# A float32 two-block network on one core: the delta-rule inverse in 64-row blocks, modulation tiles in three slots, distances on ScalarE, latent items in pairs

## The reference

```python
# layer 0, per head and chunk: (I + L) x = rhs, L strictly lower triangular
lower = where(strict, einsum("bhncd,bhnkd->bhnck", kb, k) * decay, 0.0)
sol = triangular_solve(lower, rhs, lower=True, unit_diagonal=True)
...  # then a scan over the chunks with state (dk x dv), and o -> rms_norm(o) * silu(z)

# second block: modulation of the norms
mod = silu(c) @ ada_w + ada_b            # (1024) @ (1024, 6144)

# second block: top 256 keys by an index score, logits with a bucketed bias
rel = pos_sel - pos_b
side = where(rel > 0, 16, 0); n = abs(rel)
bucket = side + (n if n < 8 else log-spaced, steps at 12, 16, 23, 32, 46, 64, 91)
logits = q . kv_sel * scale + rel_bias[bucket]
probs = softmax(logits); out = probs @ kv_sel
```

## Time and profile before

| what | us |
|---|---|
| median of three runs | 3050.55 (3041.01 to 3058.16) |
| profiled execution, time | 3044.59 |
| profiled execution, span of the core | 3042.8 |
| inverse, on PE | 263.6 to 371.0 |
| transposes, then recurrence from its first vn product | 371.0 to 377.2 to 407.3 |
| sums of squares | 407.3 to 418.3 |
| modulation columns | 418.3 to 435.0 |
| gating and memory attention, to the first product of wout0 | 435.0 to 483.5 |
| last gab unit done; first latent product; last | 2033.1; 2042.8; 2240 |

### The profile page before, as it was taken

One profiled execution on the slowest core, in us unless ns is written; L12 is line 12 of the kernel. 1 busy time (PEld: TensorE's weight loads), 2 busy tenths in 40 slices (PEclk: granted clock), 3 DMA queues, 4 the chain that ended last, 5 costly groups with the idle time before them and its releaser, 6 DMA issues.

```text
span 3042.8 us, 33737 instructions
## 1 busy us (share of the span) xinstructions
PE 2761.9 (91%) x12772; PEld 2102.7 (69%) x12772; DVE 1602.1 (53%) x2165; ACT 1029.1 (34%) x1468; POOL 1019.3 (33%) x263
## 2 busy tenths in 40 slices
PE   5999988899998788999989999889997868799997
PEld 4778966788876467888757776664445646588885
DVE  2736743543427745434353588995535477544244
ACT  3534333322222433222233444424432232332221
POOL 3345712344442013444423333330003333244442
PEclk8999978999998899999989999899997868899998
DMA  4123502222231012222323333242221213122221
GB/s 163 70 84 139 180 28 69 82 93 92 94 115 56 29 38 74 96 97 97 111 76 135 106 109 104 104 141 88 87 108 64 103 49 111 56 83 97 97 97 69
DMA packets 59768, 280.53 MB, mean 92 GB/s; under 512 B 9699, under 2 KB 11325, under 8 KB 32387
## 3 DMA queue, kind: packets, MB, share of 16 engines
q1 hardware_dynamic: 47123, 259.84, 24.7%
q10 hardware_dynamic: 12528, 19.09, 1.7%
HBM read 259.43 MB, written 19.40 MB: 92 GB/s over the span
## 4 chain that ended last, share of the span: by engine, by line
issue 55%; PE 26%; POOL 12%; DVE 3%; DMA 2%; ACT 1%; POOLq 0%; ACTq 0%; SPq 0%; DVEq 0%
POOL w_lo L2326 10%; PE banks L480 7%; PE banks L481 7%; PE banks L482 7%; POOL acc L813 2%; DMA raw<-in_W 2%; PE banks L2000 1%; ACT raw L800 1%; POOL ysd L2075 1%; PE banks L2010 1%; PE banks L2019 0%; DVE tmp L1491 0%; PE banks L1081 0%; DVE x L1494 0%; PE banks L1128 0%
## 5 line engine op out<-in xcount | busy, mean ns | idle before, releaser
L2326 POOL TENSOR_TENSOR w_lo<-raw,w_hi 128x2048 fp32r<-128x2048 f32 x186 | 861.7, 4633 | 1824.8 <-ACT w_hi L459 1740.0
L480 PE MATMUL banks<-hn_hi,w_hi 128*128 128x512 f32 (+1 forms) x2296 | 910.9, 397 | 74.3 <-DVE hn_lo L548 39.1
L481 PE MATMUL banks<-hn_lo,w_hi 128*128 128x512 f32 (+1 forms) x2296 | 909.4, 396 | 0.0
L482 PE MATMUL banks<-hn_hi,w_lo 128*128 128x512 f32 (+1 forms) x2296 | 908.8, 396 | 0.0
L459 ACT ACTIVATE w_hi<-raw 128x2048 fp32r<-128x2048 f32 x182 | 348.3, 1914 | 714.6 <-PE banks L482 680.0
L480 PEld LDWEIGHTS banks<-hn_hi,w_hi 128*128 128x128 f32 x2296 | 439.4, 191 | 200.6 <-issue 76.8
L481 PEld LDWEIGHTS banks<-hn_lo,w_hi 128*128 128x128 f32 x2296 | 439.8, 192 | 96.6 <-issue 1.0
L482 PEld LDWEIGHTS banks<-hn_hi,w_lo 128*128 128x128 f32 x2296 | 439.1, 191 | 91.4
L664 DVE TENSOR_TENSOR hid_lo<-prod,hid_hi 128x512 f32 x66 | 302.0, 4576 | 125.8 <-ACT hid_hi L637 125.8
L481 PE MATMUL banks<-hid_lo,w_hi 128*128 128x512 f32 x528 | 207.1, 392 | 0.0
L482 PE MATMUL banks<-hid_hi,w_lo 128*128 128x512 f32 x528 | 207.1, 392 | 0.0
(11 more groups left out here) (411 smaller groups left out, 3302.0 us busy)
## 6 DMA issues: line engine op xcount, KB each, us to landing
raw<-in_W SPq DMA_DIRECT2D x210, 1024.0 KB, 4.8
spill<-cs ACTq DMA_DIRECT2D x64, 256.0 KB, 3.0
oh<-codes SPq DMA_DIRECT2D x128, 128.0 KB, 2.7
grp<-spill SPq DMA_DIRECT2D x8, 512.0 KB, 4.6
grp<-spill SPq DMA_DIRECT2D x16, 256.0 KB, 5.0
zt<-spill SPq DMA_DIRECT2D x8, 512.0 KB, 3.7
x<-in_xT SPq DMA_DIRECT2D x1, 2048.0 KB, 14.7
ma<-spill SPq DMA_DIRECT2D x1, 2048.0 KB, 9.6
```

The costliest lines, as they stand in the source:

```text
L480: pe.matmul(out, wh, xh(k), start=(k == 0), stop=False)
L481: pe.matmul(out, wh, xl(k), start=False, stop=False)
L482: mm = pe.matmul(out, wl, xh(k), start=False, stop=(k == nkt - 1))
L2326: pool.tensor_tensor(w_lo[:, u % 2, :], raw[:, u % 2, :], w_hi[:, u % 2, :].bitcast(F32), ALU.subtract).then_inc(S("w_lo"), 1)
```

## The change

1. *Inverse.* The seven levels on 128 x 128 become six on the two 64 x 64 diagonal blocks of each chunk, and one last step for the block below. The upper block's products use rows and columns 0 to 63 of the array, the lower's 64 to 127; both write the same PSUM bank, other partitions. `xi`, its transpose `xb` and `zm` are stored as 4 x 64 columns a head, so each DVE operation has 256 elements in place of 512. The last step multiplies the corner of `lt` by the upper inverse, copies, multiplies by the lower one and writes the negated result into `xt`, whose lower left is filled with zeros by POOL beforehand.
2. *Modulation.* A third slot, `extra`, joins the two of `raw`; the tile i uses slot i mod 3. ACT scales 16 tiles ahead of the recurrence and two behind each of its chunks. PE forms 12 of the 48 columns where all stood, and six in each of the first six attention items. ACT rounds the next two units behind item 7's step in place of behind the gating. The banks of `modulation` and `ob` move.
3. *Buckets.* |key - query| is one ACT operation (Abs with a bias) in gate steps 17 to 20; DVE has 10 operations a block instead of 13.
4. *Latent attention.* Items go in pairs: two logits, both biases, then (every second pair) the values, then two transposes of the pair before the last; `pr2` and `st2` have four slots.

```diff
+SLOTS = 3
-                    for c in range(NC):
-                        cc = slice(c * P, (c + 1) * P)
-                        mm = pe.matmul(bank(key)[:, cc], lt[:, h, cc], xi[:, h, cc] if lv else ident[:, :],
-                                       start=True, stop=True)
+                    for c in range(NC):
+                        for b_, half in enumerate(HALF):
+                            mm = pe.matmul(bank(key)[half, c * 64:c * 64 + 64], corner(lt, h, c, b_),
+                                           xi[half, h, c, :] if lv else ident[half, half], start=True, stop=True,
+                                           skip_group_check=True)
...
+            for h in range(HG):
+                key = ("iz", 6, h)
+                open_bank(pe, key)
+                taken(pe, ("iw", 5, h))
+                for c in range(NC):
+                    mm = pe.matmul(bank(key)[high, c * 64:c * 64 + 64], lt[low, h, c * P + 64:c * P + P],
+                                   xi[low, h, c, :], start=True, stop=True)
+                mm.then_inc(fills(key), 1)
+            for h in range(HG):
+                key = ("iv", 6, h)
...
+                    mm = pe.matmul(bank(key)[low, c * 64:c * 64 + 64], zm[high, h, c, :], corner(xt, h, c, 1),
+                                   start=True, stop=True)
...
+        def ada_slot(i):
+            return extra if i % SLOTS == 2 else raw[:, i % SLOTS, :]
+        def sp_ada(sp):
+            for i in range(COUNT["ada"]):
...
+                else:
+                    sp.wait_ge(S("w_lo"), ADA + i - 2)
+                land = S("w_land2") if i % SLOTS == 2 else w_land[i % SLOTS]
+                sp.dma_start(ada_slot(i)[:, :], I["W"][ADA + i]).then_inc(land, 16)
...
+            pool.memset(xt[64:P, :, :].rearrange("p h (c n) -> p (h c) n", c=NC)[:, :, 0:64], 0.0).then_inc(S("xt_zero"), 1)
...
             (act_recurrence, in the loop over chunks)
+                act_ada(a, 16 + 2 * c, 18 + 2 * c)
-            act_after_ada(a)
             (pe_onorm)
-            pe_modulation(pe)
+            pe_modulation(pe, 0, 12)
             (pe_attention, layer 0, item n, behind the turn)
+                if layer == 0 and n < 6:
+                    pe_modulation(pe, 12 + 6 * n, 18 + 6 * n)
             (act_attention, behind the copy of the turned tile)
+                if layer == 0 and n == 7:
+                    act_after_ada(a)
             (dve_buckets)
-            step(v.tensor_scalar(rel, kp, qpc[:, 0, b:b + 1], None, ALU.subtract), 0)
-            step(v.tensor_scalar(acc, rel, 0.0, 16.0, ALU.is_gt, ALU.mult), 1)
-            step(v.tensor_scalar(dist, rel, -1.0, None, ALU.mult), 2)
-            step(v.tensor_tensor(dist, dist, rel, ALU.max), 3)
+            step(v.tensor_scalar(acc, kp, qpc[:, 0, b:b + 1], 16.0, ALU.is_gt, ALU.mult), 0)
+            v.wait_ge(S("distance"), b + 1)
+        def act_distance(a, b):
+            a.wait_ge(S("topk"), (b + 1) * (2 * RD + 5))
+            a.activation(isc(b), kp, ACT.Abs, bias=qpn[:, b:b + 1]).then_inc(S("distance"), 1)
             (act_steps)
+                if 17 <= i < 21:
+                    act_distance(a, i - 17)
```

More of the change, by code:

```diff
@@ L173, in bank_plan @@
     k.add(("onorm",), 0)
-    k.add(("modulation",), 7)
-    k.rotate([("ob", h) for h in range(HG)], [1, 2, 3])
+    k.add(("modulation",), 1)
+    k.rotate([("ob", h) for h in range(HG)], [2, 3, 4])
     attention(0)
@@ L1356, in dve_onorm @@
                                    op1=ALU.mult).then_inc(S("rows_inverse"), 1)
-            key = ("modulation",)
-            full(v, key)
-            v.tensor_tensor(mod[:, :], bank(key)[:, 0:48], mod[:, :], ALU.add).then_inc(reads(key), 1)
             for h in range(HG + 1):
@@ L1868, in pe_latent @@
                               skip_group_check=True)
-                    pe.wait_ge(S("one_hot"), n // 2 + 1)
+                if pair:
+                    pe.wait_ge(S("one_hot"), N + 1)
+                for n in pair:
+                    key = ("logit", n)
                     for part in range(3):
@@ L1938, in act_latent @@
                     a.activation(qh[:, G * T:(G + 1) * T], bank(key)[:, :], ACT.Copy).then_inc(reads(key), 1)
+                for m in (2 * N - 4, 2 * N - 3):
+                    if 0 <= m < NG:
+                        key = ("ptp", m)
+                        full(a, key)
+                        g = m % 4
+                        a.activation(ptt[:, m // 4 % 2, :, g * P:(g + 1) * P], chunked(bank(key)[:, :]), ACT.Copy)\
+                            .then_inc(reads(key), 1)
         def pe_values(pe):
@@ L2441, in _ @@
             dve_attention(v, 0)
+            key = ("modulation",)
+            full(v, key)
+            v.tensor_tensor(mod[:, :], bank(key)[:, 0:48], mod[:, :], ALU.add).then_inc(reads(key), 1)
             dve_squares(v, "wout0", to_x(v), sq_tmp)
```

229 lines of the change are left out of this document (136 added, 93 removed).

## The result

The changed kernel takes 3015.16 us (median of eleven runs, 3002.16 to 3029.45) against 3045.07 for the kernel before (3041.01 to 3058.16): a ratio of 0.990, 95% interval 0.9883 to 0.9918, or 25 to 36 us less. The forecast was 2990, in a range of 2968 to 3030. So the sign and the range held, and a good half of the expected gain is there; some 25 us of it are missing. The measured time lies above 2968 to 3005, the part of the range that the prediction gave to the forecast itself. The profiled execution took 3012.98 us with a span of 3010.8, 32.0 less than the span before.

The account below looks back on a forecast made before the run. TensorE was taken to bound the inverse, with chains or other limits elsewhere; -48.5 + 3 (+10 - 11 + 4) - 3.3 - 8 = -56.8 from 3044.6 gives 2988, set at 2990; range 2968 to 3030, the forecast itself 2968 to 3005.

Parts of the forecast that it names:

- rival (3): Inverse: the quarters overlap only partially, 0.040 to 0.050 us an instruction, 73 to 91 us; total 3002 to 3020; chance 0.07.
- rival (4): Recurrence to projection: the modulation moves, but clock and load waits cost +20 us instead of +3; total 3005; chance 0.08.
- Inverse, -48.5: Inverse: 107.4 us become 59, at 0.060 us an instruction with two quarters at once; -48.5 us.
- Rivals (1): Inverse: quarters don't overlap in one PSUM bank, 109 us, total 3038; or the clock halves, 3045; chance 0.13.
- (2): Inverse: each change of quarter drains the array, so it takes 213 us; total 3142; chance 0.06.
- Late tiles: Modulation tiles beside the inverse: with the third slot GpSimd is done by 322, before the recurrence at 328.7; no cost.
- Recurrence, +10: Recurrence: scalings between chunks save 4 us at the first chunk, cost 7.5 at boundaries and 5.5 at the end; +9, clock +1.
- The clock term: Recurrence: TensorE idles over 2 us at each chunk boundary and then runs at half clock; +1 us, bounds 0 and 6.
- Columns, -11: Sums to gating: only 24 modulation column instructions stay, so gating starts 5.7 instead of 16.7 us behind the sums; -11 us.
- attention, +4: Six attention items take 12 column instructions each, 1.3 to 2.5 us an item, less moved splits; +4 us, between 0 and +10.
- Buckets, -3.3: Bucket blocks: fewer VectorE operations, but late one-hot tiles; first one-hot product at 2041.4 instead of 2044.75; -3.3 us, bounds -9 and 0.
- Latents, -8: Latent attention: two items share one round of array changes, saving 0.27 us each, 32 x 0.27 = 8.6; -8 us, bounds -9 and +4.

Follow-up runs that it names:

- quiet: The changed kernel loading only 64 of 2048 columns of modulation tiles 4 to 23, same instructions; 3000.72 us (one run).
- second trace: The changed kernel, unedited, run and traced once more; 3017.80 us, ratio 0.9899.
- one_per_chunk: The changed kernel with modulation tiles 4 to 20 scaled ahead of the recurrence, one behind each of chunks 0 to 2, none behind the last; 3002.57 us, ratio 0.9859.
- inverse_only: The kernel before with only the 64-row inverse, its tiles, masks and zero fill; twenty scalings ahead of the recurrence as before; 3048.58 us, ratio 1.0004.
- old_inverse: The changed kernel with the inverse of the kernel before, on 128 rows; 3052.38 us, ratio 1.0027.
- late_two: The changed kernel with the last two modulation scalings moved behind the square root of the head sums; 3013.06 us, ratio 0.9888.

## Why the forecast was right, and where it was off

That the range held is in part luck. Its upper part, 3005 to 3020, was added for rival (3), a partial overlap, and rival (4), +20 from recurrence to projection. Neither came true: the quarters overlap fully, and the four stages of (4) add up to +5.5. The time came out there for reasons that the prediction did not name, taken one by one here.

**Inverse, -48.5, measured -36.0 with the turned tiles.** The step that failed is "At 0.060 for an instruction and two quarters at once: 864 x 0.060 + 96 x 0.060 = 57.6". As a price of the engine it is right to 0.3 us: quiet shows 57.3, and the pitch is (3.02 - 0.22) / 95 = 0.029 for a matmul at level 0. As the time of the stage it left out who brings 3648 instructions. In the trace before TensorE had only 1920 in 107 us, with eight of these packets and no stop, and the feed was named nowhere in the forecast, neither in the sum nor in a rival. Rival (3) gives the right size, 73 us, by the wrong mechanism (partial overlap). It should have been a term with bounds: the stage doubled its instructions and halved its time.

**Rivals (1) and (2)** are out. The two quarters write one bank at once and overlap fully (a matmul every 0.029 us, where the last step's one quarter has 0.058). The rule of the Trainium skill (TensorEngine Tiling (Array Packing), Restrictions and Gotchas) that different row tiles cannot use a bank at the same time did not bite here, where the two quarters also differ in their output partitions. Nor did the skill's 62 ns a matmul with hardware decode off (TensorE: Matmul & The Clock Gate, "Wait — 56ns, not 53.3ns?"), with a matmul and its load every 0.029. VectorE's share was right: 52.1 us busy for the 53 worked out, not the bound in the changed kernel, and close to it once the stops are gone (*quiet*).

**Late tiles.** "done by 322" was right (GpSimd ends tile 15 at 321.1). "So the slot costs nothing and pays only because the inverse is short": that slot and split together pay only then is shown from both sides by inverse_only and old_inverse. That the slot costs nothing is not shown, as it was never changed alone; with the split, old_inverse loses 9.3 us up to the projection. What it didn't see is that from 321 to 347 GpSimd had nothing to do, time for five tiles that stood behind the chunks instead.

**Recurrence, +10, measured +6.7** (9.3 in the second trace). The mechanism is right, by one_per_chunk worth 12.1. By TensorE's rows the first chunk's wait gave back 2.7 (forecast 4), the three boundaries cost 6.6 (7.5) and the end 5.4 (5.5). The clock term had the wrong sign: instead of costing 1 it gave back 2.9, since the first chunk had run at half clock only in the kernel before.

**Squares, 0, measured +5.4.** The forecast gave the cold clock 1 us, "bounds 0 and 6", and put it at the chunk boundaries. At the boundaries TensorE idled for 1.7 to 2.7 and kept the full clock (in late_two, behind 2.47, it did not); in the 6.4 us pause ahead of the first square it fell to half, and stayed there to 431. The bound held, the place and the value did not: a chain of six steps whose TensorE part is 1.07 at full clock pays 0.9 in each.

**Columns, -11, measured -11.0; attention, +4, measured +4.4 and 8.8.** Without columns in the items the stage takes 41.2, so the splits and copies that moved were worth 7.3 together (forecast 8 less 2.3, 5.7), and the columns cost 11.7 to 16.1 (1.3 to 2.5 an item were the bounds, 8 to 15). The value taken was near the low end; at a clock of 0.56 to 0.60 it belonged near the high one.

**Buckets, -3.3, measured -3.8.** Right in size; the first comparison waited for its loads (7.10 us), and GpSimd's split, which ran at the same time, only stretched it.

**Latents, -8, measured -4.6.** "32 x 0.27 = 8.6" is right for the steady part (8.3). What failed is that it was the whole: a pipeline one pair deeper ends later by 3.9.

**Second layer's attention, 0, measured +5.4.** No step of the forecast could have given it; the granted clock was 0.86 there in place of 0.91, and what brings that about stays open.

## What to carry to other kernels

Where a change makes instructions smaller and more numerous, count them against the time: how fast the program itself arrives is a term of the sum, above all beside heavy weight loads. When a path is shortened that runs beside another of nearly the same length, neither change is worth anything alone, so time both together. And of work that is moved onto an engine's queue ask two things more: how long TensorE then stands still ahead of a chain of small steps, and whether a VectorE operation with both operands in SBUF meets GpSimd there.

## What the runs showed of the hardware

- TensorE took 256 instructions in 5.0 us while 209 to 239 GB/s of weights were loaded, and stopped for 0.6 to 2.6 us after each 250 or so (changed kernel, one_per_chunk); with 12 GB/s it took 256 in 4.0, one stop of 0.2 aside (quiet, one run).
- Float32 matmul instructions of 64 x 64 on two diagonal quarters come every 0.029 us into one bank, on one quarter alone every 0.058, and they overlap also when all of one quarter's products of a bank stand in a row (0.036).
- A VectorE operation of 256 elements with both operands in SBUF took 4.41 us beside GpSimd's adds and 0.41 between two of them; its neighbour with one operand in PSUM always took 0.41.
- The granted clock fell from 1.00 to 0.50 while sums of 512 columns and one-column matmuls followed each other without a gap (a sum 1.07, then 1.97), and stayed at 1.00 when TensorE idled for 0.78 us between the same sums. Ahead of the same sums a pause of 4.8 to 9.1 us went with half clock in six kernels, one of 0.98 with full clock at the first sum in eight.
